# Band attention with the scores of heads h and h + 4 made together

## The reference

```python
def window_attn_latent(q, k, v, k_ctx, v_ctx, sink):      # 8 query heads, 2 key heads, 64 wide
    ...
    s_loc = jnp.einsum('bnqhgd,bnkhd->bnhgqk', qb, kw).astype(jnp.float32) * SCALE_A
    band = jnp.abs(kj - qi) <= WINDOW
    ...
    s_ctx = jnp.einsum('bnqhgd,blhd->bnhgql', qb, k_ctx).astype(jnp.float32) * SCALE_A
    ...
    p = jax.nn.softmax(jnp.concatenate([s_loc, s_ctx, s_sink], axis=-1), axis=-1)
    ...
    o = (jnp.einsum('bnhgqk,bnkhd->bnqhgd', p_loc, vw)
         + jnp.einsum('bnhgql,blhd->bnqhgd', p_ctx, v_ctx))
```

## Time and profile before

| | us |
|---|---|
| median of 3 runs | 3919.3 |
| lowest and highest | 3916.91, 3922.16 |
| the profiled execution's own time | 3926.21 |
| its span in the profile | 3924.3 |
| TensorE busy in the span | 3676.7 |
| VectorE busy in the span | 2169.5 |
| ScalarE busy in the span | 1419.9 |

### The profile page before, as it was taken

One profiled execution on the slowest core, in us unless ns is written; L12 is line 12 of the kernel. 1 busy time (PEld: TensorE's weight loads), 2 busy tenths in 40 slices (PEclk: granted clock), 3 DMA queues, 4 the chain that ended last, 5 costly groups with the idle time before them and its releaser, 6 DMA issues.

```text
span 3924.3 us, 54000 instructions
## 1 busy us (share of the span) xinstructions
PE 3676.7 (94%) x21015; PEld 3094.3 (79%) x21015; DVE 2169.5 (55%) x4547; ACT 1419.9 (36%) x2285; POOL 761.6 (19%) x645
## 2 busy tenths in 40 slices
PE   6989998979999997999997999999999879999997
PEld 4877886869898997999985568868888645776885
DVE  3353343598998667777874463274343345436443
ACT  3223323324444442333333452263222335425322
POOL 0000000007987864555530000000000000000000
PEclk8999999999999999999998999999999989989998
DMA  5223323458787889999971001101111210210222
GB/s 214 92 76 140 102 97 119 156 188 288 272 306 265 300 306 364 347 343 344 372 286 54 33 28 59 60 1 54 65 65 60 102 33 33 73 62 22 97 98 85
DMA packets 220555, 594.49 MB, mean 151 GB/s; under 512 B 17936, under 2 KB 101520, under 8 KB 215952
## 3 DMA queue, kind: packets, MB, share of 16 engines
q1 hardware_dynamic: 156592, 380.68, 28.3%
q0 software_dynamic: 36864, 134.23, 9.5%
q10 hardware_dynamic: 26848, 76.14, 5.1%
HBM read 530.16 MB, written 60.82 MB: 151 GB/s over the span
## 4 chain that ended last, share of the span: by engine, by line
PE 79%; DVE 9%; DMA 7%; issue 2%; ACT 2%; POOL 1%; ACTq 0%; DVEq 0%; SPq 0%
PE bank L735 62%; PE bank L934 6%; DMA WR<-in_vrows 4%; PE bank L1028 3%; PE bank L1014 3%; PE bank L901 2%; DVE WL L1502 1%; PE bank L759 1%; PE bank L796 1%; DMA rows<-in_urows,rk 1%; POOL rows L666 1%; DMA WR<-in_weights 1%; DMA rows<-in_vrows,rk 1%; DVE Rw L1763 1%; ACT WH L1119 0%
## 5 line engine op out<-in xcount | busy, mean ns | idle before, releaser
L1502 DVE TENSOR_TENSOR WL<-WR,WH 128x1024 fp32r<-128x1024 f32 x512 | 631.1, 1234 | 821.2 <-ACT WH L1119 767.2
L1119 ACT ACTIVATE WH<-WR 128x1024 fp32r<-128x1024 f32 x512 | 537.0, 1057 | 798.7 <-DMA WR<-in_weights 201.4
L735 PE MATMUL bank<-H2h,WH 128*128 128x512 f32 (+2 forms) x1624 | 578.6, 356 | 4.5 <-DVE H2l L1530 4.5
L735 PE MATMUL bank<-H2h,WL 128*128 128x512 f32 (+2 forms) x1624 | 573.6, 353 | 0.0
L735 PE MATMUL bank<-H2l,WH 128*128 128x512 f32 (+2 forms) x1624 | 573.0, 353 | 0.0
L735 PE MATMUL bank<-Hh,WH 128*128 128x384 f32 (+1 forms) x1440 | 527.5, 366 | 23.6 <-DVE WL L1502 23.5
L735 PE MATMUL bank<-Hh,WL 128*128 128x384 f32 (+1 forms) x1440 | 512.4, 356 | 0.0
L735 PE MATMUL bank<-Hl,WH 128*128 128x384 f32 (+1 forms) x1440 | 511.7, 355 | 0.0
L934 PE MATMUL bank<-ah,WH 128*128 128x384 f32 x1024 | 345.1, 337 | 35.3 <-issue 18.6
L666 POOL DMA_INDIRECT rows<-in_urows,rk x128 | 169.5, 1324 | 968.4 <-DVE rk L1788 744.4
L735 PEld LDWEIGHTS bank<-H2h,WH 128*128 128x128 f32 (+1 forms) x1624 | 307.0, 189 | 52.5 <-issue 7.7
(11 more groups left out here) (310 smaller groups left out, 5778.8 us busy)
## 6 DMA issues: line engine op xcount, KB each, us to landing
WR<-in_weights SPq DMA_DIRECT2D x498, 512.0 KB, 3.8
WR<-in_vrows SPq DMA_DIRECT2D x128, 512.0 KB, 9.2
gelu_by_expert<-geU ACTq DMA_DIRECT2D x128, 192.0 KB, 5.0
gates_by_expert<-tab ACTq DMA_DIRECT2D x24, 1024.0 KB, 6.4
geV<-gelu_by_expert SPq DMA_DIRECT2D x32, 768.0 KB, 11.8
Gt<-gates_by_expert SPq DMA_DIRECT2D x16, 1536.0 KB, 18.5
x_kept<-X ACTq DMA_DIRECT2D x2, 3072.0 KB, 8.7
X<-x_kept ACTq DMA_DIRECT2D x2, 3072.0 KB, 11.3
```

The source lines that it names most:

```text
L735: yield nc.tensor.matmul(b[0:rows, out_cols], a, r, start=n == 0, stop=n == len(pairs) - 1)
L1119: act.activation(WH[:, n % SLOTS, :, :].rearrange("p a b -> p (a b)"), WR[:, c % SLOTS, :, :].rearrange("p a b -> p (a b)"), ACT.Copy)\
L1502: v.tensor_tensor(WL[:, n % SLOTS, :, :].rearrange("p a b -> p (a b)"), WR[:, plan.splits[n] % SLOTS, :, :].rearrange("p a b -> p (a b)"), ...
```

## The change

Units of kind "A" come in pairs (heads h and h + 4, the same block). At every even step the scores of units s and s + 1 are issued, in the order part 0 of s, part 0 of s + 1, part 1 of s, part 1 of s + 1 (two products for a pair of context units); at odd steps none. The plan, TensorE and VectorE follow the same list, from the new function `scores_at`. T and Y stay where they were, a unit at each step, and so does ScalarE's program. Kind "B" keeps its order.

```diff
--- before.py
+++ after.py
@@ -131,13 +131,21 @@
 
 
     out = []
-    for h in range(HA):
+    for heads in ([(h, h + 4) for h in range(4)] if kind == "A" else [(h,) for h in range(HB)]):
         for qb in range(TX):
             lo, hi = (max(qb - 1, 0), min(qb + 2, TX)) if kind == "A" else (0, TX)
-            out.append((h, qb, lo, hi))
+            out += [(h, qb, lo, hi) for h in heads]
         if l == 0:
-            out += [(h, TX + c, 0, 0) for c in range(C // P)]
+            out += [(h, TX + c, 0, 0) for c in range(C // P) for h in heads]
     return out
+
+
+def scores_at(kind, us, s):
+
+    if s >= len(us) or (kind == "A" and s % 2):
+        return []
+    new = (s, s + 1) if kind == "A" else (s,)
+    return [(u, part) for part in (range(2) if us[s][3] > us[s][2] else (1,)) for u in new]
 
 
 def make_plan():
@@ -269,9 +277,8 @@
                 if s < n:
                     if kind == "B" and us[s][1] == 0:
                         heads(us[s][0])
-                    if us[s][3] > us[s][2]:
-                        p.job(("S", kind, l, s, 0), "V")
-                    p.job(("S", kind, l, s, 1), "V")
+                for u, part in scores_at(kind, us, s):
+                    p.job(("S", kind, l, u, part), "V")
                 if 2 <= s <= n + 1:
                     _, _, lo, hi = us[s - 2]
                     p.job(("T", kind, l, s - 2, 0), "A")
@@ -982,25 +989,25 @@
                     us = units(kind, l)
                     n = len(us)
                     for s in range(n + 3):
-                        if s < n:
-                            h, qb, lo, hi = us[s]
+                        if kind == "A" and s == 0:
+                            pe.wait_ge(qk_ready, k.next(qk_ready))
+                        if kind == "B" and s < n and us[s][1] == 0:
+                            h = us[s][0]
+                            if h == 0:
+                                project(0)
+                            if h + 1 < HB:
+                                project(h + 1)
+
+                            pe.wait_ge(qk_ready, k.next(qk_ready))
+                        for u, part in scores_at(kind, us, s):
+                            h, qb, lo, hi = us[u]
                             if kind == "A":
-                                if s == 0:
-                                    pe.wait_ge(qk_ready, k.next(qk_ready))
                                 p0 = HDA * (h // 4)
                                 q, kk = col(qA[p0:p0 + HDA, h % 4, :], qb), kA[p0:p0 + HDA, 0, :]
                             else:
-                                if qb == 0:
-                                    if h == 0:
-                                        project(0)
-                                    if h + 1 < HB:
-                                        project(h + 1)
-
-                                    pe.wait_ge(qk_ready, k.next(qk_ready))
                                 q, kk = col(QH[0:QKB, h % 2, :], qb), KH[0:QKB, h % 2, :]
-                            if hi > lo:
-                                product(("S", kind, l, s, 0), slice(0, (hi - lo) * P), [(q, kk[:, lo * P:hi * P])])
-                            product(("S", kind, l, s, 1), slice(0, C), [(q, kk[:, T:A])])
+                            keys = kk[:, T:A] if part else kk[:, lo * P:hi * P]
+                            product(("S", kind, l, u, part), slice(0, C if part else (hi - lo) * P), [(q, keys)])
                         if 2 <= s <= n + 1:
                             u = s - 2
                             _, _, lo, hi = us[u]
@@ -1970,29 +1977,28 @@
                                 project(0)
                             if us[s][0] + 1 < HB:
                                 project(us[s][0] + 1)
-                        if s < n:
-
-                            h, qb, lo, hi = us[s]
+                        new = scores_at(kind, us, s)
+                        if s >= 4 and new:
+                            old = new[-1][0] - 4
+                            lo4, hi4 = us[old][2:]
+                            dve.wait_ge(filled, k.filling(filled, ("T", kind, l, old, 1 if hi4 - lo4 > 2 else 0)))
+                        for u, part in new:
+                            h, qb, lo, hi = us[u]
                             nl = (hi - lo) * P
-                            W = nl + C
-                            m = s % 8
-                            row = Srow[kind][s % 4]
-                            if s >= 4:
-                                lo4, hi4 = us[s - 4][2:]
-                                old = ("T", kind, l, s - 4, 1 if hi4 - lo4 > 2 else 0)
-                                dve.wait_ge(filled, k.filling(filled, old))
+                            row, m = Srow[kind][u % 4], u % 8
                             low_ = V("sink", l * 8 + h) if kind == "A" else NEG
-                            parts = ([(0, 0, nl)] if nl else []) + [(1, nl, C)]
-                            for part, at, n_ in parts:
-                                b = bank_of(("S", kind, l, s, part))
-                                if kind == "A" and part == 0:
-                                    m0 = (lo - qb + 1) * P
-                                    add = band[:, m0:m0 + nl]
-                                else:
-                                    add = band[:, P:P + 1].to_broadcast([P, n_])
-                                v.tensor_tensor_reduce(row[:, at:at + n_], b[:, 0:n_], add, scale, low_, ALU.add,
-                                                       ALU.max, mx[:, m, part:part + 1])\
-                                    .then_inc(dve_read, k.inc(dve_read))
+                            at, n_ = (nl, C) if part else (0, nl)
+                            b = bank_of(("S", kind, l, u, part))
+                            if kind == "A" and part == 0:
+                                m0 = (lo - qb + 1) * P
+                                add = band[:, m0:m0 + nl]
+                            else:
+                                add = band[:, P:P + 1].to_broadcast([P, n_])
+                            v.tensor_tensor_reduce(row[:, at:at + n_], b[:, 0:n_], add, scale, low_, ALU.add,
+                                                   ALU.max, mx[:, m, part:part + 1])\
+                                .then_inc(dve_read, k.inc(dve_read))
+                            if not part:
+                                continue
                             dve.wait_ge(*k.own())
                             if nl:
                                 v.tensor_scalar(nm[:, m:m + 1], mx[:, m, 1:2], mx[:, m, 0:1], -1.0, ALU.max, ALU.mult)\
```

## The result

The changed kernel takes 3869.0 us (median of 4 runs, 3861.0 to 3876.8) against 3920.7 for the kernel before (median of 4): 51.7 us less, a ratio of 0.9862 with an interval of 0.9832 to 0.9892. The direction was right, the size was not.

The account below looks back on a forecast made before the run. The band stages were taken as bound by PE's own work, with DVE next. Gains of 15 us in layer 0 and 16 in layer 1, together 31 us off the median 3919.3, gave 3888 us; range 3876 to 3911.

Parts of the forecast that it names:

- The overlap: Band-attention scores on PE: products in different row halves overlap fully, so a pair costs one unit's 1.27, 1.06 or 0.63 us.
- DVE late next: Band stages: DVE bounds edge and context pairs (3.76, 2.84 us); two heads take 21.7 us in layer 0, 16.1 in layer 1.
- The hand-over: PE waiting for DVE's reading of PSUM banks between pairs: priced at nothing, at most 0.3 us over 40 pairs, 12 us.
- (a): Score pairs overlap only as a chain in strict order, middle pair 1.59 us: 6 us lost, 3894; chance 0.10.
- (b): Row halves of the score products do not overlap; only one 0.20 us start per pair is saved, 8 us, 3911; chance 0.10.
- (d): Band stages slower because holes in PE keep the clock at 1.2 GHz: 3973 us at worst; chance 0.06.
- (c): PE, DVE and ACT wait in turn at each pair: 12 us of the 31 lost or somewhat more, 3901; chance 0.10.
- to the last tenth: Reading of the profile before: PE is busy without idle time in all four windows of the two band stretches.
- I let the spell be as long as today: Low-clock spells at the start of the band stretches keep their 15 us (layer 0) and 34 us (layer 1).
- (e): Layer 1's low-clock spell shortens to 15 us because more of the array works: 9 us more gain, 3879; chance 0.2.

Follow-up runs that it names:

- kernel before without spells: Kernel before plus two extra 384-wide float32 products, result unused, in TensorE's 1.5 us wait at the start of each band stage: 3896.8 us, ratio 0.9931.
- same-half kernel: Changed kernel with pairs of heads h and h + 1, both in one half of the rows, batches of four kept: 3904.8 us, ratio 0.9948.
- With the hole: Changed kernel with eight extra VectorE instructions, so TensorE waits 7.3 us in place of 1.5 ahead of each band stage: ratio 0.9917 to the kernel before.
- own step: Changed kernel with heads h and h + 4 still in turn, but each unit's scores issued separately, not in batches of four: 3909.8 us, ratio 0.9939.
- kernel before with a hole: Kernel before with eight extra VectorE instructions, so TensorE waits 7.3 us in place of 1.5 ahead of each band stage: median 3939.9 us, ratio 1.0042.

## Why the prediction was wrong in size

Right, step by step. **The overlap:** full, as taken from the value products; the groups came to 1.28, 1.06 and 0.63 us against 1.27, 1.06 and 0.63. **DVE late next:** two heads of layer 0 take 22.15 us against 21.7, and the stages at the full clock 87.9 and 65.4 us against 4 x 21.7 = 87 and 4 x 16.1 = 64. Against the kernel before without spells, 101.7 and 79.6, this is 28 us, where the same sums gave 4 x (25.5 - 21.7) + 4 x (20.0 - 16.1) = 31. The rule of the Trainium skill on the emptying of PSUM (TensorEngine Tiling, Performance Considerations) agrees with the trace: DVE waits 1.3 us for PE in layer 0, where it waited 19. **The hand-over**, priced at 0 with a bound of 12, came to about 2 us in all (153.4 us of stages against 151), in pieces such as the 2.02 us one above. Rivals (a), (b) and (d) did not happen, and (c), with its 12 us, did not either. One reading was loose: in layer 0 PE is not busy "to the last tenth" but idle for 0.2 us in each window, which changes nothing.

The step that failed is "I let the spell be as long as today". With it I gave the low-clock part a gain of its own from the halved scores but kept its 15 and 34 us. The kernel before loses 22 us to its spells (203.4 us of stages against 181.3 without them), the changed one next to nothing, and 28 + 22 = 50 us is the difference of the stages, 203.4 to 153.4. By my sum 31 us had been given to both together. The price of the spells stood in the rows: 108 and 95 us of stage against four times 25.5 and 20.0. I used it only to confirm the sum of today. Of the 28 us at the full clock, one start per pair saved by the batch is about 8 (2.35 us for a middle pair against twice 1.27, 40 pairs), and the overlap the rest. Of the 22 us of spells, the same-half kernel already saves about 13 by the estimate above.

Two things came together in "next to nothing". With the hole the changed kernel leaves the low clock after 4 or 5 us, and without it the clock did not fall at all in layer 0 of its first profile and in both layers of the second, behind the same wait of 1.47 us. The prediction had no term for the second, and no run here says how often it happens.

Rival (e) had the direction, a spell that ends sooner, but in layer 1 only, with 15 us left and a chance of 0.2, worth 9 us. Its reason, more of the array at work, is not shown to be the main one. The bottom of the range, 3876, was made from it "with a little for other spells". With no spell in either layer the prediction's own sums give 87 + 64 = 151 us of stages in place of 203.4, 52 us less, and so 3867; 3869 was measured. The evidence for weighing it higher was in the trace: a PE that was never idle and yet stayed at the low clock for 34 us in layer 1, and for 14 in layer 0, so that the length of a spell was not given by PE being busy and had no reason to stay as it was under another order. I put that fact under rival (d), as a reason why the clock might stay low.

## What to carry to other kernels

Where a stage stands at the low clock with a busy TensorE, price the spell as a term of its own (stage length against the full-clock rate of the same trace), and give the forecast of a change that reorders such work two values, with the spell kept and with it gone. Two extra products in a hole of 1.5 us ahead of such a stage were worth 27 us in the kernel before, half of what the change brought, and are to be tried first; in the changed kernel, which had lost its spells, they brought nothing that can be measured (3868.2 against 3869.4 us). When products that use half of the rows overlap, the next limit is read from the idle-free loop of the engine that empties the banks; here it gave the stages to 2% (151 us against 153.4).

## What the runs showed of the hardware

Score products of 64 rows in different halves overlap in full, and the order in the program within a batch of four does not matter: 1.13 us alternating, 1.14 us with both lower ones first. The Trainium skill (TensorE: Matmul & The Clock Gate, Packing small matmuls) has matmuls strictly in order at start and end; by that rule the second order would have overlapped only at its seam, an estimated 1.8 us for an edge pair (1.99 us without overlap less one record of 0.2), and the measurement decides.

A TensorE without a pause can stay at the low clock for long: 39 and 73 us in the profiled execution of the kernel before with a hole, with PE busy in 39.00 of 39 and 72.88 of 73 us; with the halves overlapped, 4 and 5 us, and with the same batches in one half, 19 and 11 us.

After a wait of 1.47 us the clock fell in some executions (the kernel before, both layers) and not in others (own step, both layers). With the wait filled the ten runs of the kernel before lie at 3891 to 3902 us, where none of its 25 own runs does.
